# Scores of two differential rounds in one burst of four row groups, behind the transposes and value step of the first

## What is computed

```
def diff_attend(q, k, v, qpos, kpos, lam):
    s = jnp.einsum('bqhcd,bkhcd->bhcqk', q, k)
    p = masked_softmax(s, kpos[None, :] <= qpos[:, None])
    a = p[:, :, 0] - lam * p[:, :, 1]
    return jnp.einsum('bhqk,bkhv->bqhv', a.astype(v.dtype), v)

def window_attend(q, k, v, qpos, kpos):
    s = jnp.einsum('btgrd,bsgd->btgrs', q, k)
    p = masked_softmax(s, mask[None, :, None, None, :])
    return jnp.einsum('btgrs,bsgd->btgrd', p.astype(v.dtype), v)
```

## Time and profile before

| | us |
|---|---|
| median of 3 runs | 878.2 (876.43 to 880.44) |
| the profiled execution | 880.67 |
| its span, first to last instruction | 878.8 |
| mean granted TensorE clock | 0.937 |
| HBM read / written | 214.72 MB / 10.04 MB |

### The profile page before, as it was taken

How to read it: one execution, slowest core, us unless ns; L and a number is a source line. 1 busy time by engine, 2 the same in 40 slices (tenths; PEclk the granted TensorE clock), 3 DMA queues, 4 the chain that set the end, 5 groups by cost and what they waited for, 6 DMA issues and landing times.

```text
span 878.8 us, 14940 instructions
## 1 busy us (share of the span) xinstructions
PE 792.2 (90%) x4891; PEld 381.3 (43%) x4891; DVE 451.8 (51%) x980; ACT 189.3 (22%) x484; POOL 19.7 (2%) x38
## 2 busy tenths in 40 slices
PE   6999999899988799999999998897888867887998
PEld 2555544355343434454535662342433323335443
DVE  2133234354305438678536357575775673584923
ACT  1310020001002002122224213242342341243000
POOL 0000000000000100010001010000000000000000
PEclk9999999999999989999999978898978897997999
DMA  9987697969979697978683179995788888682011
GB/s 343 319 260 220 243 364 252 378 222 335 338 248 352 217 354 265 352 259 331 224 265 128 37 249 307 333 307 186 229 281 271 269 266 293 221 353 120 1 48 50
DMA packets 136873, 221.62 MB, mean 252 GB/s; under 512 B 17482, under 2 KB 65779, under 8 KB 135323
## 3 DMA queue, kind: packets, MB, share of 16 engines
q1 hardware_dynamic: 113930, 197.40, 65.3%
q10 hardware_dynamic: 20528, 14.27, 5.3%
q0 software_dynamic: 2336, 8.99, 3.1%
HBM read 214.72 MB, written 10.04 MB: 256 GB/s over the span
## 4 chain that ended last, share of the span: by engine, by line
PE 62%; SPq 14%; DVE 11%; DMA 9%; issue 4%; ACT 0%; ACTq 0%; DVEq 0%
PE banks L591 13%; PE banks L613 13%; SPq L383 9%; PE banks L1031 6%; PE banks L627 4%; PE banks L844 4%; PE banks L559 3%; DMA proj<-in_cmp_cache 3%; DVE att L1714 2%; PE banks L874 2%; DMA ring<-in_dv_cache 2%; DMA ring<-in_dk_cache 2%; PE banks L912 2%; PE banks L890 2%; SPq L378 2%
## 5 line engine op out<-in xcount | busy, mean ns | idle before, releaser
L613 PE MATMUL banks<-ring,xt 128*128 128x512 f32 x448 | 199.7, 599 | 0.0
L613 PEld LDWEIGHTS banks<-ring,xt 128*128 128x128 f32 x448 | 83.4, 191 | 104.7 <-issue 104.6
L1261 ACT ACTIVATE wide<-banks,att 128x128 f32<-128x128 f32 (+3 forms) x128 | 66.3, 523 | 179.8 <-DVE att L1714 174.3
L591 PE MATMUL banks<-proj,wide 128*64 128x256 f32 x896 | 102.2, 390 | 1.7 <-DMA proj<-in_cmp_cache 1.7
L844 PE MATMUL banks<-ring,small 128*32 128x512 f32 x512 | 80.0, 705 | 20.7 <-DMA ring<-in_dv_cache 17.9
L591 PEld LDWEIGHTS banks<-proj,wide 128*64 128x64 f32 x896 | 65.2, 141 | 40.9 <-DMA proj<-in_cmp_cache 7.0
L627 PE MATMUL banks<-ring,small 128*32 128x512 f32 x512 | 62.8, 612 | 16.9 <-DMA ring<-in_dk_cache 16.9
L1439 DVE TENSOR_SCALAR small<-small 128x510 f32<-128x510 f32 x8 | 3.4, 426 | 143.5 <-ACT small L1100 128.6
L1085 ACT ACTIVATE proj<-banks,x_rs 128x512 f32<-128x512 f32 x32 | 22.0, 687 | 216.4 <-PE banks L613 207.1
L890 PE MATMUL banks<-consts,wide 128*128 128x128 f32 x240 | 45.4, 317 | 16.9 <-DVE xt L1738 8.8
L874 PE MATMUL banks<-proj 32*128 32x128 f32 (+7 forms) x256 | 59.6, 546 | 0.0
(11 more groups left out here) (342 smaller groups left out, 812.4 us busy)
## 6 DMA issues: line engine op xcount, KB each, us to landing
ring<-in_dk_cache SPq DMA_DIRECT2D x256, 256.0 KB, 5.9
ring<-in_dv_cache SPq DMA_DIRECT2D x256, 256.0 KB, 4.0
proj<-in_cmp_cache SPq DMA_DIRECT2D x144, 128.0 KB, 3.9
ring<-in_w_in SPq DMA_DIRECT2D x7, 2048.0 KB, 10.0
proj<-in_cmp_cache ACTq DMA_DIRECT2D x80, 128.0 KB, 5.6
ring<-in_x_nat SPq DMA_DIRECT2D x2, 2048.0 KB
ring<-in_cmp_cache SPq DMA_DIRECT2D x32, 128.0 KB, 3.8
ring<-in_w_out SPq DMA_DIRECT2D x1, 4096.0 KB, 12.4
```

What stands on the lines that cost most here:

```text
L591: last = mm(to, w1[:, kv, half, lp, :], rows[:, kv, g, lp, :, :, :], start=lp + half == 0, stop=lp == LP - 1 and half == 1, tile_position= ...
L613: last = mm(banks[:, 3 + n % 2, :], xt[:, k, P * t:P * t + P], w_ring[:, c % 2, k, :], start=k == 0, stop=k == KC - 1)
L1261: last = A(e_slot(j, c)[:, 0:n], banks[:, 2 * (j % 2) + c, 0:n], ACT.Exp, bias=row_max[:, j % 4, c:c + 1], accum_out=row_sum[:, j % 4, c:c ...
```

## The change

The scores of kinds 0 and 1 are issued together, in the round of kind 0, after that round's transposes, its pick and its value step, and before the selected attention's steps. They wait for the exponentials of j-1 instead of those of j-2. The scores of kinds 2 and 3 stay where they were. VectorE copies the picked sums before it masks the scores of the round, since the value step now stands ahead of those.

```
+            def scores_pair(j):
+
+                if j > 0:
+                    pe.wait_ge(s("exps"), j)
+                else:
+                    pe.wait_ge(s("proj_kept"), 32)
+                    pe.wait_ge(s("turned_kept"), N_TURNS)
+                    pe.wait_ge(s("win_vector"), step("win_read"))
+                score_products(j)
+                score_products(j + 1)
...
             for j in range(DUOS + 4):
...
-                if j < DUOS:
+                if j < DUOS and j % 4 > 1:
                     scores_of(j)
...
                 if j + V_EARLY < 64:
                     v_step(j + V_EARLY)
+                if j < DUOS and j % 4 == 0:
+                    scores_pair(j)
                 for n in range(2):
                     if j == SEL_AT[n]:
                         sel_scores(n)
...
                 if j < DUOS and j % 8 == V_EARLY:
                     mask_v(j // 8)
+                if j < DUOS and j % 8 == V_EARLY:
+                    keep_v(j // 8)
                 if j < DUOS:
                     mask_max(j)
-                if j < DUOS and j % 8 == V_EARLY:
-                    keep_v(j // 8)
                 if 1 <= j < DUOS + 1:
                     scale(j - 1)
```

More of the change, by code:

```diff
@@ L857, in _, with score_products @@
             last.then_inc(s("win_tensor"), 1)
-            def scores_of(j):
+            def score_products(j):
                 r, tp, t, kind, n = duo(j)
[L862 to L868, removed]
                 for c in range(2):
@@ L876, in scores_of @@
                 last.then_inc(s("scored"), 1)
+            def scores_of(j):
+                pe.wait_ge(s("exps"), j - 1)
+                score_products(j)
[6 more added lines that the diff above has]
+                    pe.wait_ge(s("win_vector"), step("win_read"))
+                score_products(j)
+                score_products(j + 1)
             def turn(j):
```

## The result

The changed kernel takes 911.66 us (median, 908.83 to 914.36), beside 878.82 (876.43 to 880.44) for the kernel before on the same chip: ratio 1.0373, 95% interval 1.033 to 1.0415. It is slower, as forecast, but by 32.8 us where 15.5 were forecast, and it lies outside the range. The profiled execution took 912.29 us (span 910.4).

What follows compares the result with a forecast made beforehand. The joint loop is bound by turns by a ring of TensorE, VectorE and ScalarE and by the page stream; quads' 13.5 us plus 2.0 for the clock give 15.5 on the 878.2 median: 894 us, range 880 to 908.

Steps and rivals of the forecast that it cites:

- the first links of the mechanism: Rounds 4g: VectorE's mask starts 2.8 us later at 128 columns, delaying the scaling and then TensorE's transposes, which lose 2.0.
- the term for the clock: Joint loop: added TensorE idling brings one more half-clock stretch, 2.0 us, between -3 and +8.
- the price of a quad: Each four rounds of the joint loop lose 2.1 us at 128 columns, 2.3 at 256 and 384, 2.6 at 512.
- as late as the round, not later: ScalarE's queue in round 4g: the copy of j-2 behind the late exponentials is delayed only as much as the round.
- The page cover: Page waits of 4.6 and 13.3 us cut quads 1-2 from 4.6 to 1.5, quads 7-12 from 14.0 to 3.
- Quads 5, 6, 13, 14: Selection stretches: 5 and 13 cost 0, between -2 and +2, as selection scores cover the delay; 6 and 14 cost 1.0 each.
- the second, 910 (0.13): Rival: quads 1, 2 and 7 to 12 pay in full, plus 5 for the clock: 32.6 us added; chance 0.13.
- The page rival at 882: Rival: page waits hide quads 1 and 2 and all but 0.7 us of 7 to 12, about 882; chance 0.16.
- The third, TensorE's time: Rival: TensorE's time decides, packing the scores takes off 13.0 us, of which some 8 show: 870; chance 0.09.
- the wait for the exponentials of j-1: Ahead of the late pair: waiting for these instead of those of j-2 costs nothing, as they end before.
- Signs forecast: Changed trace, quads without page waits: mask of 4g 2 to 4 us later, transposes of 4g-1 wait about 2, among others.

Runs made afterwards that it cites:

- e8: Changed kernel plus two extra 128x512 products into a free bank ahead of the transposes of rounds 4g+1, in twelve quads: 895.92 us.
- e1: Changed kernel, but the pair of scores is issued at the head of round 4g, ahead of transposes and value step: 880.04 us.
- e3: Changed kernel, but in rounds 4g VectorE scales j-1 and copies j-2 ahead of the late mask: 903.61 us.
- e4: As e3, and ScalarE too copies j-2 ahead of the late exponentials of round 4g: 898.42 us.
- e13: Changed kernel with both the VectorE and ScalarE orders of e4 and the extra products of e8: 890.11 us.
- e14: Changed kernel, but the pair is issued behind the transposes and the pick and ahead of the value step: 888.77 us.
- e6: Changed kernel with two of the four value pages of each step loaded, output left incomplete: 910.49 us.
- e5: Kernel before the change with two of the four value pages of each step loaded, output left incomplete: 859.4 us.
- e2: Changed kernel unpaired: scores of kind 0 alone go behind transposes and value step, kind 1 stays at the head of its round: 918.9 us.

## Why the prediction was right and wrong

Start of the maximum of round 4g+3, the last of a quad, before and after, and the growth between the lines beside the terms forecast:

| to the end of quad | before | after | late | growth | forecast |
|---|---|---|---|---|---|
| 2 | 561.3 | 564.5 | 3.2 | 3.2 | 1.5 |
| 4 | 593.6 | 604.6 | 11.0 | 7.8 | 4.7 |
| 6 | 633.1 | 648.2 | 15.1 | 4.1 | 1.0 |
| 12 | 738.7 | 763.9 | 25.2 | 10.1 | 3.0 |
| 15 | 791.5 | 824.7 | 33.2 | 8.0 | 3.3 |
| clock, in no quad | | | | | 2.0 |

**The direction, and the first links of the mechanism, were right.** The late mask pushes the scaling, the scaling the transposes. The added idle time of TensorE that is a delay, 33.2 us, lies ahead of the transposes of rounds 4g-1, where the prediction said that it must. At 128 columns the mask was 2.8 late by forecast; it waits 2.68. From the mask's start to the end of the scaling 1.98 were forecast and 592.48 - 590.40 = 2.08 measured.

**The step that failed most is the term for the clock.** The prediction prices one more half stretch at 2 us and says "I take one: 2.0, between -3 and +8". The runs put some 16 us there: e8 gives 15.7 back, and between e1 and the changed kernel TensorE's busy time for the same products grows by 17.7. It is no term beside the price of a quad but a factor on it. Behind each of the eleven waits TensorE is found at half clock, at the latest in the value step: in round 16 transposes and value step take 1.78 and 1.94 us, where the same two took 1.07 and 1.06 just before, and of the ten value steps behind such waits all take 1.44 to 1.94 us, where before the change four of the same ten took 1.06 or 1.07. I counted one stretch because I took the 14 us of idle time as a sum and not as eleven separate waits. The Trainium skill, "TensorE: Matmul & The Clock Gate", Part 1, puts the ramp at under 1% of a typical kernel's span; this is said of the first products of a kernel, and its section "HAM oscillation" says that the cost is paid again with each gap that brings the half clock back. The trace agrees with the second: 15.7 of 911.7 us (1.7%) were given back by products that add 30.5 us of work.

**The second is the price of a quad.** It rests on the sentences that TensorE's next transposes wait for just that scaling, and that ScalarE's copy of j-2 comes "as late as the round, not later". The transposes of 4g-1 wait for three things, and two of them I had put behind the mask myself without following them on to TensorE: VectorE's copy of 4g-2 and ScalarE's copy of 4g-2, behind two exponentials of the late round. In the three waits at 128 columns VectorE's copy comes last (2.85 us where some 2.1 was forecast, 8.6 together), in the eight at 256 to 512 columns ScalarE's (2.51 to 3.70, 26.0 together). The eleven waits are 33.2 us more than before, where the terms of the same eleven quads were 4.6 + 4.7 + 14.0 + 2.3 = 25.6, 7.6 too little. e3 and e4 show what both orders are worth together: 13.2 of the missing 17.3, but about half of it through the clock. The worths overlap, as e13 shows, and don't add up. I also priced the value step ahead of the pair at its 1.0 us, in ten quads; e14 shows 22.9, since the same step, issued a place later, fills the wait.

**The page cover was right, and a little small.** My terms before any cover, 4.6 + 4.7 + 1 + 14.0 + 1 + 2.3 + 2 = 29.6, stood against 51.1 measured (e6 less e5); the cover I took was 3.1 + 11.0 = 14.1, and 18.3 was measured (16 by the ratios, so that "too small" is within the noise). Page waits went from 17.9 to nothing, where I wrote under 8. The error of 17.3 is 21.5 too little in the price (some 14 to 16 of it the clock, 7.6 the waits, within the noise of these differences) less 4.2 too little in the cover.

**Quads 5, 6, 13, 14.** Quads 5 and 6 together grew by 4.1, not 1.0. The selection scores do run beside both masks, as forecast, but the mask of 20 came late for a reason that the term left out:

```profile
615.04 1.24 PE L867 MATMUL banks<-proj 32*128 32x256 f32 x8
616.21 4.15 PE L943 MATMUL banks<-ring,q_sel 128*32 128x512 f32 x16
616.31 0.43 DVE L1724 TENSOR_TENSOR banks<-banks,consts 128x256 f32<-128x256 f32 x1 [3.28 <-PE banks L867]
```

It waits 3.28 us behind a pick, a value step of 1.93 and a pair of 1.24 at half clock.

**The rivals.** The time fell to the second, 910 (0.13), but not by its mechanism: it had the pages hide nothing, and they hid some 18, and it had 5 us for the clock. That its sum is near is an accident of two errors. The page rival at 882 had the cover right and the price too small. The third, TensorE's time, falls by e1: packing alone moves nothing, though it takes 15.8 us of products off, since the wait for the exponentials comes in their place; behind the late place it is worth 7 us (e2), where TensorE is what the late mask waits for. I had put the wait for the exponentials of j-1 at nothing, which is right at the late place: no such wait stands ahead of the pair there.

**Signs forecast.** Right: the mask of 4g waits 2 to 4 us (2.68, 2.32, 3.28; 1.85 to 3.96 in quads 1 to 15), that of 4g+1 in no quad; four products abreast took 0.50 and 1.14 us (forecast 0.49 and 1.15 to 1.2). Wrong: the transposes of 4g-1 wait 2.51 to 3.70 us, not about 2, and in quads 5, 6, 13 and 14, where other work stands between, not at all. The waits of VectorE's masking addition did not become fewer. They went from 61.9 to 87.4 us in 37 places with a longest of 5.7, where it had been 35 and 6.9; in rounds 4g from 2.9 to 43.4, in rounds 4g+1 from 16.9 to none. The loop ended 31.7 us later, not about 15.

## What to carry to other kernels

When a step is moved back in one engine's program, follow all that stands behind its consumers in their own queues, not only the next step, and ask of each who waits for it: here the copies that free TensorE's banks stood behind the late work, on two engines, and taking them out of there gave 13 us back. Price a repeated wait of TensorE with the half clock that follows it, wait by wait, and before you call a gain a shorter wait, see whether the idle time or the busy time fell; whether the clock is in the loss can be tried with products into a free bank, and the same products in a kernel without these waits are the control, if its other waits stay as they were. And a block of work that waits for no one (the value step) belongs behind a block that others wait for.

## What the runs showed of the hardware

Four products in four row groups run abreast: 1.14 us at 512 columns where two took 1.13, and 0.50 at 128 where two took 0.49. Products without any use, 30.5 us of them, made a kernel 15.7 us faster, and 29.6 us of them cost another one at most 0.6%, part of them in place of page waits. The same products took TensorE 215.71 us of busy time in one order and 233.41 in another, with 74 and 120 us at half clock. Which share of the 15.7 is clock and which is a shift in when the engines meet was not tried apart; the time at half clock fell by 54 us with it.
